# Position mix of a gated MLP layer: three 128-column matmuls into one bank a group, in place of a 256- and a 128-column one into two banks

## The reference

```
x: (1, 2048, 1024) float32; 8 groups of 128 channels, chunks of 128 positions
def mixer_chunked_sgu(h, w_in, v_g, w_s, b_s, w_out):
    z = gelu(h @ w_in);  u, v = split(z, 2)
    v = rmsnorm(v, v_g)                        # (16 chunks, 128 s, 8 g, 128 c)
    ws = where(lower triangle, w_s, 0)         # (8 g, 128 t, 128 s)
    s = einsum('gts,bnsgc->bntgc', ws, v) + b_s.T
    return (u * s) @ w_out
x = x + mixer(rmsnorm(x));  x = x + relu(rmsnorm(x) @ w1)**2 @ w2;  return rmsnorm(x)
```

## Time and profile before

| What | Value |
|---|---|
| median of 3 runs | 1829.41 us (1825.41 to 1831.1) |
| profiled execution, its time | 1824.81 us |
| its span, first to last instruction | 1823.1 us |
| PE busy | 1793.9 us, 98% of the span |
| PEld busy | 1489.6 us, 82% |
| DVE busy | 1112.3 us, 61% |
| ACT busy | 783.6 us, 43% |
| POOL busy | 419.2 us, 23% |
| mean granted TensorE clock | 0.998 |

### The profile page before, as it was taken

How to read it: one execution, slowest core, us unless ns; L and a number is a source line. 1 busy time by engine, 2 the same in 40 slices (tenths; PEclk the granted TensorE clock), 3 DMA queues, 4 the chain that set the end, 5 groups by cost and what they waited for, 6 DMA issues and landing times.

```text
span 1823.1 us, 20050 instructions
## 1 busy us (share of the span) xinstructions
PE 1793.9 (98%) x8088; PEld 1489.6 (82%) x8088; DVE 1112.3 (61%) x1121; ACT 783.6 (43%) x871; POOL 419.2 (23%) x390
## 2 busy tenths in 40 slices
PE   7999999999999999999999999999999999999998
PEld 5888888888888888888878888888888888888886
DVE  3483475386175765655676656674666666866665
ACT  5534535525533644343643443353433335333332
POOL 2442442441342123330012112210242202000001
PEclk9999999999999999999999999999999999999999
DMA  8656665765754788885957777799977655755552
GB/s 332 244 220 241 246 230 189 260 242 195 274 188 174 272 279 285 284 278 185 353 190 265 257 234 229 277 398 307 308 269 277 231 208 194 278 185 191 208 201 93
DMA packets 134301, 445.40 MB, mean 244 GB/s; under 512 B 8384, under 2 KB 9408, under 8 KB 118464
## 3 DMA queue, kind: packets, MB, share of 16 engines
q1 hardware_dynamic: 105584, 328.75, 51.6%
q0 software_dynamic: 25168, 92.80, 14.1%
q10 hardware_dynamic: 3456, 22.56, 3.2%
HBM read 318.26 MB, written 125.83 MB: 244 GB/s over the span
## 4 chain that ended last, share of the span: by engine, by line
PE 92%; DVE 4%; DMA 1%; ACT 1%; issue 1%; ACTq 0%; POOL 0%; POOLq 0%; DVEq 0%
PE bank L1229 65%; PE bank L1067 26%; DMA w_raw<-in_a_w_out 1%; PE bank L1089 1%; DVE w_lo L804 1%; PE bank L1113 1%; DVE yT_lo L880 1%; DVE uT L875 0%; DVE biased L864 0%; ACT yT_hi L612 0%; DVE uT L843 0%; DMA gains<-in_a_v_g 0%; DVE biased L870 0%; DVE Y L1003 0%; ACT w_hi L554 0%
## 5 line engine op out<-in xcount | busy, mean ns | idle before, releaser
L1229 PE MATMUL bank<-x_hi,u_hi 128*128 128x512 f32 x896 | 349.9, 390 | 4.6 <-DVE c L976 2.1
L1229 PE MATMUL bank<-x_lo,u_hi 128*128 128x512 f32 x896 | 349.3, 390 | 0.0
L1229 PE MATMUL bank<-x_hi,u_lo 128*128 128x512 f32 x896 | 349.1, 390 | 0.0
L1229 PE MATMUL bank<-d_hi,a_hi 128*128 128x512 f32 x896 | 348.5, 389 | 0.0
L1229 PE MATMUL bank<-d_lo,a_hi 128*128 128x512 f32 x896 | 348.5, 389 | 0.0
L1229 PE MATMUL bank<-d_hi,a_lo 128*128 128x512 f32 x896 | 348.5, 389 | 0.0
L976 DVE TENSOR_TENSOR Y<-bank,Y 128x512 f32<-128x512 f32 x208 | 137.8, 687 | 175.8 <-PE bank L1229 175.5
L810 DVE TENSOR_TENSOR u_lo<-u_raw,u_hi 128x1024 fp32r<-128x1024 f32 x112 | 155.5, 1396 | 144.7 <-ACT u_hi L559 144.1
L564 ACT ACTIVATE d_hi<-d_raw 128x2048 fp32r<-128x2048 f32 x56 | 107.4, 1919 | 286.1 <-DMA d_raw<-w2sum 159.9
L804 DVE TENSOR_TENSOR w_lo<-w_raw,w_hi 128x2048 fp32r<-128x2048 f32 x47 | 117.9, 2521 | 168.8 <-ACT w_hi L554 159.8
L1229 PEld LDWEIGHTS bank<-x_hi,u_hi 128*128 128x128 f32 x896 | 168.5, 188 | 41.4 <-DVE u_lo L810 4.3
(11 more groups left out here) (108 smaller groups left out, 2702.6 us busy)
## 6 DMA issues: line engine op xcount, KB each, us to landing
a_raw<-a2s SPq DMA_DIRECT2D x56, 1024.0 KB, 7.7
a2s<-sums SPq DMA_DIRECT2D x32, 1280.0 KB, 8.2
job<-in_mlp_w POOLq DMA_DIRECT2D x32, 1024.0 KB, 8.2
u_raw<-w1sum SPq DMA_DIRECT2D x64, 512.0 KB, 4.7
d_raw<-w2sum SPq DMA_DIRECT2D x32, 1024.0 KB, 4.9
w_raw<-in_a_w_in SPq DMA_DIRECT2D x31, 1024.0 KB, 6.3
u_raw<-in_mlp_w SPq DMA_DIRECT2D x48, 512.0 KB, 5.2
d_raw<-in_mlp_w SPq DMA_DIRECT2D x24, 1024.0 KB, 5.2
```

Of the source, the lines that this page charges most:

```text
L1229: ins = pe.matmul(bank_of(g, j)[:, :], stationary[x_part][:, k, j * P:(j + 1) * P], moving[y_part][:, k, :], start=i in (0, 1, 3) and k == ...
```

## The change

`mix` issues for each chunk the three passes one by one, each with 128 moving columns, all three into the same 128 columns of one bank, so that TensorE adds all the parts. A group takes one bank, four chunks side by side, and a pair two banks; `mix_bank` rotates over four banks, and a pair waits on `mix_read` only for the pair before the last. `gate` reads the bank once, in one instruction of 512 elements, in place of four of 256.

```
-        def mix_bank(q, g, i):
-            return bank_set(q, MIX)[2 * (g % 2) + i]
+        def mix_bank(q, g):
+            return bank_set(q, MIX)[g % 4]
...
             def gate(q, g):
                 dve.wait_ge(mix_done, q * G + g + 1)
                 to = biased[:, g % 2, :].rearrange("p (n t) -> p n t", t=P)
-                banks = [mix_bank(q, g, i)[:, :].rearrange("p (n h t) -> p n h t", h=2, t=P) for i in range(2)]
-                for i in range(2):
-                    dve.scalar_tensor_tensor(
-                        out=to[:, 2 * i:2 * i + 2, :], in0=banks[i][:, :, 0, :], scalar=g_v[:, g:g + 1],
-                        in1=bias_rows[:, g:g + 1, :].to_broadcast([P, 2, P]), op0=ALU.mult, op1=ALU.add)\
-                        .then_inc(mix_biased, 1)
-                for i in range(2):
-                    dve.wait_ge(mix_biased, 2 * (q * G + g) + i + 1)
-                    dve.scalar_tensor_tensor(
-                        out=to[:, 2 * i:2 * i + 2, :], in0=banks[i][:, :, 1, :], scalar=g_v[:, g:g + 1],
-                        in1=to[:, 2 * i:2 * i + 2, :], op0=ALU.mult, op1=ALU.add).then_inc(mix_read, 1)
-                dve.wait_ge(mix_read, 2 * (q * G + g + 1))
+                dve.scalar_tensor_tensor(
+                    out=to, in0=mix_bank(q, g)[:, :].rearrange("p (n t) -> p n t", t=P), scalar=g_v[:, g:g + 1],
+                    in1=bias_rows[:, g:g + 1, :].to_broadcast([P, TT, P]), op0=ALU.mult, op1=ALU.add)\
+                    .then_inc(mix_read, 1)
+                dve.wait_ge(mix_read, q * G + g + 1)
                 dve.wait_ge(u_gelu, q * G + g + 1)
...
             def mix(q, g):
                 for t in range(TT):
-                    to = mix_bank(q, g, t // 2)[:, t % 2 * 2 * P:(t % 2 + 1) * 2 * P]
-                    pe.matmul(to, vn[q % 2][HI][:, t, g * P:(g + 1) * P],
-                              wsT[:, g, :, :].rearrange("p h t -> p (h t)"), start=True, stop=False,
-                              skip_group_check=True)
-                    ins = pe.matmul(to[:, 0:P], vn[q % 2][LO][:, t, g * P:(g + 1) * P], wsT[:, g, HI, :],
-                                    start=False, stop=True, skip_group_check=True)
+                    for n, (x_part, y_part) in enumerate(PASSES):
+                        ins = pe.matmul(mix_bank(q, g)[:, t * P:(t + 1) * P],
+                                        vn[q % 2][x_part][:, t, g * P:(g + 1) * P],
+                                        wsT[:, g, y_part, :], start=n == 0, stop=n == 2)
                 ins.then_inc(mix_done, 1)
...
-                    pe.wait_ge(mix_read, 2 * (q * G + g))
+                    if g >= 4:
+                        pe.wait_ge(mix_read, q * G + g - 2)
...
-                pe.wait_ge(mix_read, 2 * (q * G + G))
+                pe.wait_ge(mix_read, q * G + G)
```

More of the change, by code:

```diff
@@ L193, in build @@
         v_hi_done, v_ready = sem("v_hi_done"), sem("v_ready")
-        mix_biased, mix_read, y_done = sem("mix_biased"), sem("mix_read"), sem("y_done")
+        mix_read, y_done = sem("mix_read"), sem("y_done")
         y_hi_done, y_ready = sem("y_hi_done"), sem("y_ready")
```

## The result

The changed kernel takes 1835.65 us (median of 11 runs, 1833.44 to 1840.41) against 1827.62 us (median of 11, 1825.41 to 1831.1) for the kernel before. The ratio is 1.0045 with a 95% interval of 1.0036 to 1.0054: slower by 0.45%, some 8.2 us (6.6 to 9.9). The forecast was +8.3 us.

What follows compares the result with a forecast made beforehand. TensorE, busy 98% of the span, was taken to bound the kernel. Mix pairs +12.3 us less 4.0 us of regained waits gave +8.3 us, 1837.7 us against the median of 1829.41; range 1831 to 1843.

Steps and rivals of the forecast that it cites:

- What bounds the kernel: Whole kernel: TensorE, busy 98% of the span, sets the time; other engines count only where TensorE waits for them.
- A chunk's price before: Old mix on TensorE: a chunk step takes 231 ns, two matmuls with two loads; a pair of groups takes 1.85 us.
- The lower bound: Changed mix: 104 ns per load with matmul, from load spacing, 2.50 us a pair, +10.4 us over 16 pairs.
- A chunk's price after: Changed mix: three loads with matmuls at 109 ns, 327 ns a step, 2.62 us a pair, +12.3 us over 16 pairs.
- The bounds of 104 and 115.5: Changed mix: lowest and highest price in ns of a load with its matmul, +10.4 to +14.7 us over 16 pairs.
- The waits: TensorE's three waits for DVE's scale_u in the blocks: recorded 3.4 us, expected to disappear and give back 4.0 us.
- The reason put first: At the scale_u waits: DVE's gates become 0.91 us shorter each, 2.7 us over three gates against a wait of 1.47.
- The edit priced at nothing: Mix pairs on TensorE: looser mix_read waits give nothing, since no wait for mix_read is recorded.
- Rival 1: Changed mix: every load with matmul costs half an old step, 115.5 ns; +10.7 us with waits regained, 1840.1; chance 0.22.
- Rival 2: Changed mix: columns count and loads hide, at or below 77 ns a matmul; -4.0 us, 1825.4; chance 0.12.
- rival 3: Changed mix: only the repeated pass is short, 70 ns, the others 109; +3.3 us with the waits, 1832.7; chance 0.07.
- A new wait: At scale_u(q, 1): DVE 2.7 us later than reckoned puts a new wait in; up to +12.3 us, 1841.7; chance 0.05.

Runs made afterwards that it cites:

- e2_long_gate: The changed kernel with DVE's gates lengthened to 1.57 us by two extra reads that add nothing; ratio 1.0057 to the kernel before.
- e3: The changed kernel with passes ordered hi*hi, lo*hi, hi*lo, so no two matmuls in a row share a stationary part; one execution, 1838.95 us.
- e4: The changed kernel with 64 moving columns per pass in place of 128, all loads kept; one execution, 1839.36 us.
- e5: The kernel before with each chunk's second matmul also 256 columns wide, still two loads a step; one execution, 1830.98 us.
- e1: The kernel before with only DVE's order changed: scale_u(q, 1) runs between gate 3's reads and its multiply; ratio 1.0010 to the kernel before.
- e7: The kernel before with scale_u(q, 1) ahead of gate 3's multiply and mix pair 6 one k later; 1824.04 us against 1827.39, ratio 0.9972.
- e6: The kernel before with its mix kept and gates that leave out adding the second halves, 0.87 us a gate; ratio 0.9968 to the kernel before.
- e8: The kernel before with only mix pair 6 moved one k later in the first output unit; ratio 1.0004 to the kernel before.

## Why the prediction was right, and where it was off

**What bounds the kernel.** Right: TensorE's own work and its three waits are 9.4 of the ruler's 9.7 us. e2_long_gate, with DVE's gates at 1.57 us for 0.79 and nothing changed in the ruler, is the plainest proof.

**A chunk's price before.** The reading that a step is one interval of a load and one slightly longer held. The split was off: 104 ns by the spacing of the load records left 127 for the other, while the experiments give 112 (e3, e4 and the changed kernel) and 120 (e5). Most of the error is rounding. The rows have two decimals, and seven intervals in a steady rhythm are rounded alike; in the trace's nanoseconds the same spacing is 108.6 in every one of the 16 pairs, and 121.6 behind 256 columns. The lower bound that was taken from it, +10.4, should have stood at 24 x 108.6 = 2.61 us a pair, +12.1.

**A chunk's price after.** The mechanism was right, the price a little too small: 112 ns, where 109 was taken from the transposes, whose weight loads are another kind in the records (0.14 us for 0.19). It made the pairs +12.3 in place of +13.4, 8% less. The bounds of 104 and 115.5 enclosed it. That adding three times into the same columns stalls nothing was left at zero, and the rows agree: the 21 intervals above, of which two in three lead to a matmul that adds, have 111 or 112 ns each with 64 columns.

**The waits.** The sum of 4.0 us was right within 0.3: pairs at +13.4 and a ruler of +9.7 leave 3.7, and the three steps with a wait took 4.0 us more than the others in the kernel before. The reason put first was not the one that acted alone. By e2_long_gate TensorE's lateness of 2.5 us at the first output unit covers a loss of 1.67 at most without any help from DVE. The prediction had named this lateness behind the word "moreover"; had it asked what the shorter gate is worth once the mix is longer, it would have found nothing.

**The edit priced at nothing.** No wait for `mix_read` is recorded before or after, as forecast; the looser wait was not tried by itself. But e1 showed that the strict one of before was met only 0.4 us ahead of time, and that "no wait recorded" did not mean slack.

**The rivals.** Rival 1, all loads at 115.5 ns: the 112 measured lies midway between it and the forecast's 109, and the ruler's +9.7 is nearer to its +10.7 than to +8.3. What speaks against it is its reason, that a step of before is two equal halves: 112 and 120 in runs of equal width make up the 231. Rival 2, columns alone, at 77 to 81 ns a matmul, and rival 3, half of that by the repeated part: refuted by e4 and e3. A new wait: none in the changed kernel. The difference of the medians was met within 0.3 us, and this is in part luck: by the ruler the blocks cost 9.7, 1.4 above the forecast. The time itself was forecast 2.0 us too high (1837.7), since the median of before, taken from three runs, was 1.8 above that of eleven.

## What to carry to other kernels

Count matmuls with their loads, not columns, when matmuls get narrow: at 128 columns one matmul with its load took 112 ns, at 256 it took 120, so a 256-column matmul does double the work for 8 ns more, and replacing it by two of 128 cost 104 ns. Let an accumulation on TensorE replace work on another engine only if TensorE waits for that engine, and ask whether the longer work on TensorE has not by itself swallowed the wait. When a wait is removed, look for the semaphore that was satisfied just in time behind it; here it took back the whole gain until the waiting instruction was moved too. And be careful with a mean of rounded times in a steady rhythm: all of them can be rounded the same way.

## What was not expected of the hardware

**The granted clock behind a short pause.** In e5_lo_256 a wait of 2.2 us was followed by a stretch at a mean granted clock of 0.76, and one of 1.47 us in the kernel before was not. At the start of the MLP the changed kernel has the same thing behind a pause of 2.0 us, by its windows:

```profile
594.38:605.26 10.88, 10.88 (x49) 1.00 0.92 367
607.20:614.50 7.30, 7.27 (x26) 0.77 0.97 385
628.00:640.00 12.00, 12.00 (x59) 1.00 0.73 242
```

In the profiled execution of the kernel before, the same 24 matmuls behind a pause of 1.6 us ran at the full clock:

```profile
597.10:602.80 5.70, 5.67 (x25) 1.00 1.01 397
```

From start to start the 24 matmuls behind the pause take 7.1 us and 5.6, which is 1.6 us of the 3.2 that the two profiled executions differ by in the MLP. The lower clock isn't bound to the changed mix (e5 and e7 show it with the mix of before, e2 has the changed mix without it), and the length of the pause doesn't decide it. All ten profiled executions have a pause at this place. In nine of them it is 1.96 to 2.17 us long; five of these (the changed kernel, e3, e4, e5, e7) went on at a mean granted clock of 0.76 to 0.77 and four (e1, e2, e6, e8) at 1.00, the shortest pause among the five and the longest among the four. It helps to explain why single executions scatter by several microseconds, and why the ruler over the blocks told more than one time did. What decides it is left open.

**How little the columns cost behind a load.** 64 columns in place of 128 left the interval at 112 ns. The chain of e4_64_columns has a run of 33 matmuls of 512 columns just ahead of its pair (start us, us, what):

```profile
79.78 7.48 PE bank L1059 x33
```

That is 227 ns each. By the column a cycle of 2.4 GHz that the prediction worked out, 512 columns stream in 213 ns and 256 in 107; the intervals of 227 and 120 are each some 13 ns more than that, while those of 128 and 64 columns stay at 112. So the price of a matmul with its load here is the larger of 112 ns and its columns with 13 ns on top, an estimate from these four widths.
